# Gating four of eight one-hot tokens on ScalarE in a PEER expert block, with the gathered slots respread

## The reference

```python
def peer_ffn(h, w_query, sub_keys, expert_u, expert_v):
    qry = (h @ w_query).reshape(T, P_HEADS, 2, P_HALF)
    scores = jnp.einsum("thcd,hcnd->thcn", qry, sub_keys).astype(jnp.float32)
    s_top, i_top = lax.top_k(scores, P_TOPK)
    ...
    gates = jax.nn.softmax(best_s, axis=-1).astype(h.dtype)
    ...
        act = jax.nn.gelu(jnp.einsum("td,thkd->thk", hb, expert_u[eb]), approximate=False)
        return jnp.einsum("thk,thkd->td", act * gb, expert_v[eb])
```

## Time and profile before

| what | value |
|---|---|
| median of 3 runs | 2018.15 us |
| lowest, highest | 2016.12 us, 2018.7 us |
| span of the profiled execution | 2011.3 us |
| median less span | 6.85 us |
| u stage (from the first L1994 to the last) | 844.1 to 1477.4 us |
| hot steps 60 to 107 in it | 1103 to 1389 us |
| granted TensorE clock, mean | 0.989 |

### The profile page before, as it was taken

The page is one execution under the profiler, slowest core; times in us unless marked ns, Lnnn a source line. Parts: engine busy times, 40 slices in busy tenths (PEclk is TensorE's granted clock), DMA queues, the critical chain, the costliest instruction groups (busy, mean ns, idle before and its releaser), DMA issues.

```text
span 2011.3 us, 27895 instructions
## 1 busy us (share of the span) xinstructions
PE 1937.0 (96%) x10341; PEld 1714.5 (85%) x10341; DVE 1489.4 (74%) x2727; ACT 719.0 (36%) x1324; POOL 481.5 (24%) x240
## 2 busy tenths in 40 slices
PE   5999998999999989999999999999999999999998
PEld 3889776889877888899999999999988888888886
DVE  5677445364475545787889999997689889899895
ACT  4110234010252243344443444444444444444443
POOL 0443202343213113100111521111222323332221
PEclk9999999999999999999999999999999999999999
DMA  6335511354212422257767688888999999999993
GB/s 253 105 106 182 172 54 48 106 191 147 63 43 73 158 80 88 72 173 255 234 225 241 231 318 297 299 296 300 412 395 401 401 400 398 400 398 401 400 375 115
DMA packets 212642, 467.99 MB, mean 233 GB/s; under 512 B 13576, under 2 KB 157120, under 8 KB 193344
## 3 DMA queue, kind: packets, MB, share of 16 engines
q1 hardware_dynamic: 194112, 332.54, 47.6%
q0 software_dynamic: 18432, 134.23, 16.9%
HBM read 412.19 MB, written 54.53 MB: 232 GB/s over the span
## 4 chain that ended last, share of the span: by engine, by line
PE 52%; DVE 2%; DMA 2%; ACT 1%; issue 0%; POOLq 0%; POOL 0%; SPq 0%; ACTq 0%; DVEq 0%
PE xin_out L2038 26%; PE xin_ps_u L1994 22%; PE xin_out L2016 4%; DMA con_raw<-in_expert_u 2%; DVE in_ulo L2156 1%; ACT in_uhi L2067 0%; DVE experts_rows L1787 0%; DVE experts_acc L1806 0%; DVE over_s_stage L2170 0%; ACT L2109 0%; ACT over_v_vhi L2074 0%; DVE over_v_vlo L2305 0%; POOLq L95 0%; POOL xin_x L2147 0%; DVE over_s_stage L2253 0%
## 5 line engine op out<-in xcount | busy, mean ns | idle before, releaser
L1780 POOL DMA_INDIRECT experts_rows<-in_expert_rows,experts_idx x128 | 247.3, 1932 | 873.2 <-DVE experts_acc L1806 738.4
L1994 PE MATMUL xin_ps_u<-con_h_hi,in_uhi 128*128 128x384 f32 x1024 | 349.0, 341 | 9.4 <-DVE in_ulo L2156 7.2
L1994 PE MATMUL xin_ps_u<-con_h_hi,in_ulo 128*128 128x384 f32 x1024 | 343.3, 335 | 0.0
L1994 PE MATMUL xin_ps_u<-con_h_lo,in_uhi 128*128 128x384 f32 x1024 | 343.3, 335 | 0.0
L2038 PE MATMUL xin_out<-over_v_vhi,xin_whi 128*128 128x512 f32 x768 | 239.1, 390 | 2.1 <-DVE xin_wlo L2307 2.0
L2038 PE MATMUL xin_out<-over_v_vhi,xin_wlo 128*128 128x512 f32 x768 | 238.8, 390 | 0.0
L2038 PE MATMUL xin_out<-over_v_vlo,xin_whi 128*128 128x512 f32 x768 | 238.5, 390 | 0.0
L2156 DVE TENSOR_TENSOR in_ulo<-con_raw,in_uhi 128x1024 fp32r<-128x1024 f32 x127 | 155.5, 1224 | 78.3 <-ACT in_uhi L2067 75.9
L488 POOL TENSOR_TENSOR weights_wlo<-con_raw,weights_whi 128x2048 fp32r<-128x2048 f32 x32 | 147.5, 4609 | 251.9 <-DVE weights_whi L561 251.9
L1994 PEld LDWEIGHTS xin_ps_u<-con_h_hi,in_uhi 128*128 128x128 f32 x1024 | 193.1, 189 | 13.7 <-DVE in_ulo L2156 11.1
L1994 PEld LDWEIGHTS xin_ps_u<-con_h_lo,in_uhi 128*128 128x128 f32 x1024 | 193.2, 189 | 0.0
(11 more groups left out here) (344 smaller groups left out, 3742.4 us busy)
## 6 DMA issues: line engine op xcount, KB each, us to landing
con_raw<-in_expert_u SPq DMA_DIRECT2D x128, 512.0 KB, 4.7
con_raw<-in_expert_v SPq DMA_DIRECT2D x128, 512.0 KB, 12.0
con_raw<-in_w_in SPq DMA_DIRECT2D x38, 1024.0 KB, 6.0
act_scratch<-in_act SPq DMA_DIRECT2D x128, 192.0 KB, 2.4
experts_hot<-act_scratch SPq DMA_DIRECT2D x128, 192.0 KB, 11.8
gate_scratch<-in_stage SPq DMA_DIRECT2D x12, 1024.0 KB, 7.1
gate_scratch<-over_s_stage SPq DMA_DIRECT2D x12, 1024.0 KB, 7.7
experts_hot<-gate_scratch SPq DMA_DIRECT2D x16, 768.0 KB, 14.1
```

The costliest lines, as they stand in the source:

```text
L1780: pool.indirect_dma_start(out=self.rows[:, r % ROWS, :], out_offset=None, in_=table, in_offset=at).then_inc(self.row_in[r % ROWS], 16)
L1994: mm = pe.matmul(ps_u[s % 2][:, 0:TD], a[s % 2][:, k, :], m[:, k, P:T], start=(i == 0), stop=(i == 3 * KD - 1))
```

## The change

Three edits. VectorE's gate multiplication (L2294) covers only tokens 4 to 7 of each hot step. ScalarE multiplies tokens 0 to 3, with one Copy activation of 128 x 128 for each, whose scale is the token's column of `slot[2]`; this stands in ScalarE's step after `cut(n + 1)` and the slot's two tiny operations, ahead of Gelu, and waits for `is_row`. TensorE waits for a new semaphore `hot_scaled` in addition to `hot_done`. The third edit moves slots within the u stage: steps 24 to 52 keep three (24, 36, 48) of eight, steps 56 to 59 keep four, the hot steps have 29 instead of 24 (n = 60, 62, 64, 65, 67, 69, 70, 72, ..., 104, 105, 107: three of every five), and from 108 on nothing changes. The total stays 51, and the v stage's slots are the same.

```diff
--- before.py
+++ after.py
@@ -1573,6 +1573,7 @@
 
 
 U_RING, R_STEPS, G_STEPS, G_TOK = 4, 12, 16, 8
+G_ACT = 4
 TD = T - P
 ND = TD // P
 SLOTS = PH * TOPK
@@ -1824,7 +1825,7 @@
     inside = [[] for n in range(NEXP)]
     r = 0
     for n in range(N_SEARCH + R_STEPS + 4, NEXP):
-        if (n < N_ROUTE and n % 4 == 0) or N_ROUTE <= n < N_HOT0 or (N_HOT0 <= n < N_HOT0 + N_HOT and n % 2 == 0) or (n >= N_HOT0 + N_HOT and n % 4 != 3):
+        if (n < N_ROUTE and n % 12 == 0) or N_ROUTE <= n < N_HOT0 or (N_HOT0 <= n < N_HOT0 + N_HOT and (n - N_HOT0) % 5 in (0, 2, 4)) or (n >= N_HOT0 + N_HOT and n % 4 != 3):
             inside[n].append(r)
             r += 1
     outside = [[] for n in range(NEXP)]
@@ -1905,7 +1906,7 @@
         block = al.block()
         assert N_TAIL > 0 and N_TAIL % 4 == 0
         STAGES, RANKS = 10, 9
-        closed, summed = al.sem("closed"), al.sem("summed")
+        closed, summed, hot_scaled = al.sem("closed"), al.sem("summed"), al.sem("hot_scaled")
 
         @block.sync
         def _(sp):
@@ -2008,6 +2009,7 @@
 
             def gates(gi, q):
                 m = G_STEPS * gi + q
+                pe.wait_ge(hot_scaled, m + 1)
                 pe.wait_ge(hot_done, m + 1)
                 for b in range(2):
 
@@ -2082,6 +2084,8 @@
                 if n > 0:
                     for r in IN_AT[n - 1]:
                         got.weigh(act, r)
+                if N_HOT0 <= n < N_HOT0 + N_HOT:
+                    scaled_rows(n - N_HOT0)
                 if n == NEXP - 1:
                     for h in range(2):
                         act.wait_ge(flushed[h], 64 * (N_HOT // G_STEPS))
@@ -2090,6 +2094,14 @@
 
                 wait(act, kept[n % 4], 16 * (n // 4))
                 act.activation(act_t[n % 4][:], ps_u[n % 2][:, 0:TD], ACT.Gelu).then_inc(gelu_done, 1)
+
+            def scaled_rows(m):
+
+                act.wait_ge(is_row, m + 1)
+                for t in range(G_ACT):
+                    row = hot_i[m % 2][:, t, :]
+                    op = act.activation(row, row, ACT.Copy, scale=slot[2][:, m * G_TOK + t:m * G_TOK + t + 1])
+                op.then_inc(hot_scaled, 1)
 
             def gates(gi, q):
                 m = G_STEPS * gi + q
@@ -2291,7 +2303,8 @@
                 dve.tensor_tensor(hot_i[m % 2], keys, i_s, ALU.is_equal).then_inc(is_row, 1)
                 dve.tensor_tensor(hot_j[m % 2], keys, j_s, ALU.is_equal)
                 dve.wait_ge(is_row, m + 1)
-                dve.tensor_tensor(hot_i[m % 2], hot_i[m % 2], g_s, ALU.mult).then_inc(hot_done, 1)
+                own = slice(G_ACT, G_TOK)
+                dve.tensor_tensor(hot_i[m % 2][:, own], hot_i[m % 2][:, own], g_s[:, own], ALU.mult).then_inc(hot_done, 1)
 
             def weighted(n):
                 s = n % RING
```

## The result

The changed kernel takes 2019.3 us (median of 12 runs, 2016.15 to 2023.24); the kernel before, run 12 times, takes 2014.55 us (2012.47 to 2018.7). The ratio is 1.0023, 95% interval 1.0014 to 1.0031: slower by 0.23%, 4.7 us. The forecast was no change, with 2017.1 us. The three runs of before shown ahead of the prediction (median 2018.15) lay high in their own spread, so the forecast's 2017.1 started from a base 3.6 us too high; the change itself was forecast as -1.1 us and measured as +4.7. That 2019.3 lies within the stated 2013.5 to 2021.0 is luck: the high base made up for it. Counted from that base of 2018.15 the range is -4.7 to +2.9 us, and the measured +4.7 lies outside.

What follows compares the result with a forecast made beforehand. TensorE was taken as the floor, 5.95 us a hot step. Span 2011.3 - 0.3 (start of hot steps) - 0.8 (behind them) = 2010.2, plus 6.85 to the median, gave 2017.1 us; range 2013.5 to 2021.0.

Steps and rivals of the forecast that it cites:

- What bounds the kernel: Hot steps: TensorE's matmuls set the 5.95 us period; VectorE runs 4% ahead of that pace.
- The half multiplication: VectorE, hot steps: 512 elements take 0.69 us, saving 0.53 us a step, worth nothing by itself.
- the five slots in: VectorE, hot steps: 2.34 us a slot, 11.7 us for five, fits under TensorE's time; effect 0.
- the five out: Routing steps: VectorE's 11.7 us there turn into more waiting for ScalarE; value 0.
- ScalarE's rows: Hot steps, ahead of Gelu: four rows take 1.41 us and fit a 2.00 us hole; cost 0.
- TensorE's added wait: Hot steps, one more wait met in time: taken as 0, at most 3.8 us in all.
- The start of the hot steps: Steps 60 to 62: the shorter multiplication gives back 0.3 us lost to late VectorE; gain 0 to 0.3 us.
- Behind the hot steps: From 1389 on, around blocks 110 and 111: moved fetches change DMA sharing; -0.8 us, between -4.4 and +2.6.
- The two signs of being wrong: Hot steps: TensorE waiting for the new activation, or the 5.95 us period moving at all, would refute the forecast.
- The sum: Whole kernel: span 2011.3 - 0.3 - 0.8 = 2010.2 us, plus 6.85 us from span to median, gives 2017.1 us.

Runs made afterwards that it cites:

- run 12: Not a label but part of "run 12 times": the kernel before, unchanged, was run 12 times, median 2014.55 us.
- experiment 11: experiment 10 without the split, VectorE multiplying all eight tokens: 2025.23 us, ratio 1.0043 to the kernel before.
- experiment 1: The changed kernel with the old slots, so the split alone: 2017.95 us, ratio 1.0013 to the kernel before.
- experiment 7: The changed kernel with 36 hot slots, five slots back in the routing steps and three behind the hot steps: 2013.45 us, ratio 0.9996 to the kernel before.
- experiment 4: The kernel before with only slots 104 and 106 moved to 105 and 107: 2019.0 us, ratio 1.0016.
- experiment 5: The kernel before with slot 112's fetch also waiting until block 109's rest tile is cut: 2018.18 us, ratio 1.0017.
- experiment 3: The changed kernel with hot slots from step 100 on at even steps and one more at 78: 2018.46 us, ratio 1.0013 to the kernel before.
- experiment 6: The changed kernel with 36 hot slots and 8 behind them, not 15: 2014.57 us, ratio 1.0001 to the kernel before.
- experiment 9: The changed kernel with the last four flushes at steps 112, 114, 116, 118: 2014.28 us, ratio 1.0000 to the kernel before.
- experiment 10: experiment 7 with the last four flushes at 112, 114, 116, 118, not 109, 112, 115, 118: 2006.79 us, ratio 0.9957 to the kernel before.
- experiment 2: The kernel before with the new slots, VectorE multiplying all eight tokens: 2024.54 us, ratio 1.0033.

## Why the prediction was wrong

*What bounds the kernel.* Right. The hot steps are TensorE's matmuls at 5.95 us, with or without the split, at 24 and at 29 slots (not at 36 without it, experiment 11).

*The half multiplication, the five slots in and the five out.* Right: 0.69 us forecast for 512 elements, 685 ns measured; 285.44 us for the hot steps; the routing steps equal to 0.1 us, in both directions (experiments 1 and 7). The rest tile is ready 2.9 us before TensorE needs it by the rows cited, not 2.4, which makes the same argument stronger. The balance of 4.54 and 2.34 us for a bare step and a slot also gave experiment 11 within 1.2 us of 302.

*ScalarE's rows.* Right in effect, 10% too dear: 0.39 us each and 1.27 us for four, where I took 0.42 and 1.41. The trace of the kernel before did have a 128 x 128 activation with one pointer, though one that reads from PSUM (`attn_p` at L1148, 363 ns). The busy time they add was forecast as 192 x 0.42 = 81 us, without the overlap that the same paragraph had worked out; the group's 60.9 us is 48 x 1.27. The Trainium skill's "ScalarE: Activation LUTs" (section on what ACT_TABLE_LOAD costs) puts 186 ns and 0.833 ns per element on an activation, 93 ns on each pointer operand, and 93 ns of overlap between neighbours. An estimate from its figures is 186 + 107 + 93 = 386 ns for one; the trace's 390 ns, and 1.27 us for four, agree.

*TensorE's added wait.* Right: none seen.

*The start of the hot steps.* Right: step 62 takes 5.94 us, not 6.25.

*Behind the hot steps.* This step failed. It named the mechanism (slot 107's accumulation releases its fetch after 1393, not 1387.7, into a stretch where the DMA engines are full) and took -0.8 us, with +2.6 as the worst. Measured: +4.5 us by steps. Two things were off. I followed the fetch to the next two blocks, 110 and 111, and these did gain: steps 109 and 110 went from 12.7 to 11.95 us, nearly the 0.8 forecast (in experiments 4 and 5 to 10.5 and 10.0). The bill came at block 113, whose load stands behind the second 1 MB flush. Its issue held SP for 5.4 us, not 2.1, and all later loads stood behind it. And I bounded the loss by the megabyte's own 2.6 us. Experiment 5 prices one megabyte, 4.8 us later, at 4.7 us net in the steps from 108 to 127 (3.4 us by its ratio, 1.8 to 5.2) and 8.0 us in steps 112 and 113 alone. The stall itself and TensorE's lower clock behind it are both in that; how they divide wasn't measured. The release was foreseen well: on the clock of the kernel before the fetch came at 1393.5, forecast 1393.7. The two signs of being wrong that I named, a wait for the new activation and another period of the hot steps, both stayed away; neither looked at the stretch that failed.

*The sum.* About 1.9 us lie between an execution's time and its span in the runs that give both (1.7 to 2.9; the profiled one of the changed kernel has 2019.59 and 2017.8), not 6.85. The rest was three high runs set against a span from another execution.

*What stays open.* In the three kernels with 29 or 36 slots in the hot steps, the last of them at 106, and the first flush at 109 (experiments 3, 6, 7), steps 109 and 110 take 15.0 to 15.7 us; in the kernel before, twice, and in experiment 1 they take 12.7. Experiment 3 has the same fetches and loads as experiment 1 from step 101 on. Why it is 2.3 us slower there wasn't settled (not by a backlog, as the DMA engines were idle just before in both), nor why experiment 1's runs lean 0.13% to the slow side while its steps are 0.7 us shorter. That the wait for the last staging copy is what makes the stall at 109 and 110 rests on experiments 9 and 10, where moving the flush took it away whole, and on the 6 us before it in which the DMA engines of the kernel before moved nothing. The late flushes in the kernel before, with nothing else changed, were not run.

## What to carry to other kernels

A change that moves work between engines also moves the moment at which buffers come free, and so when transfers start; follow each moved release to the transfers issued in the next ten or fifteen microseconds, on every queue, not only to the first one, and look for a load behind a big store in an in-order queue. Offloading an engine that isn't the bound is worth nothing alone, but the room can be filled: here with gathers taken out of a stretch where the DMA engines were full. Where an in-order queue waits for the last result of a stage, put the loads of the next stage ahead of that wait; here that alone gave nothing (experiment 9, ratio 1.0000), the room alone gave nothing (experiment 7, 0.9996), and the two together gave 0.43%.

## What the runs showed of the hardware

- Issuing a 512 KB load took SP 0.4 to 0.9 us in most places, and longer directly behind a 1 MB flush with a fetch under way: 2.08 and 3.30 us in the kernel before, 5.39 and 6.98 in the changed kernel, 4.99 and 7.33 in experiment 5, 8.10 in experiment 2. What is behind it in SP's program waits too. A long issue doesn't make a stall by itself: after those of 6.98 and 7.33 us (block 116) no step was longer than 4.16 us at that block.
- The data of an indirect fetch began to move only when GpSimd's instruction for it was over: instructions ended at 1388.7 in the kernel before, 1387.8 in the changed kernel and 1391.4 in experiment 2, and the DMA engines, idle until then, began to move data at about 1389, 1388 and 1392 (in the last with the flush, issued at the same time).
- GpSimd's instruction for one indirect fetch took 1.68 us in most places, 6.22 us in five early hot steps of the kernel before, where VectorE's timeline shows no pause (it shows one of 0.17 us every other step later, where the fetch is back at 1.68), 3.42 us in every third fetch of the changed kernel's hot steps from 1146 on, and 6.22 us in 20 of the 32 fetches that experiment 2 issued between 1100 and 1392. As the rows are fetched four slots ahead, no engine waited for them in the hot steps; but a long instruction makes the transfer late, and in experiment 2 that may be what put it onto the load of block 110.
